# Last down projection of a hybrid trunk computed in two parts of the tokens (320, then 256), with the final norm of the first part beside the second

## The reference, cut to what matters

```
h = rmsnorm(x, p["ffn_norm"][layer])
up = h @ p["w_up"][layer]
c, fb = causal_dwconv(up, ffn_bufs[layer], p["ffn_conv_w"][layer], p["ffn_conv_b"][layer])
x = x + (jax.nn.silu(c[..., :D_FF]) * c[..., D_FF:]) @ p["w_down"][layer]
...
y = rmsnorm(x, p["final_norm"])
```

## Time and profile before

| | |
|---|---|
| median of three runs | 1219.53 us (1217.68 to 1220.73) |
| the profiled execution's own time | 1217.85 us |
| its span in the trace | 1216.1 us |
| TensorE matmul busy | 1186.7 us, 98% of the span |
| VectorE, ScalarE, GpSimd busy | 734.8, 514.8, 615.8 us |
| first matmul of the last down projection | 1159.37 us into the span |
| its last matmul's result taken by VectorE | 1201.60 us |
| last store issued | 1209.31 us |

### The profile page before, as it was taken

How to read it: one execution, slowest core, us unless ns; L and a number is a source line. 1 busy time by engine, 2 the same in 40 slices (tenths; PEclk the granted TensorE clock), 3 DMA queues, 4 the chain that set the end, 5 groups by cost and what they waited for, 6 DMA issues and landing times.

```text
span 1216.1 us, 21634 instructions
## 1 busy us (share of the span) xinstructions
PE 1186.7 (98%) x8636; PEld 1156.6 (95%) x8636; DVE 734.8 (60%) x1468; ACT 514.8 (42%) x881; POOL 615.8 (51%) x628
## 2 busy tenths in 40 slices
PE   7999999999999999999999999999999999999996
PEld 7887899999999999999999999999999999999996
DVE  5999556567845688455512754355785557855542
ACT  6333455444334454343522533344443444533354
POOL 4643435347954469542454323434588355874430
PEclk9999999999999999999999999999999999999998
DMA  6311134221342203422422222322223221232212
GB/s 239 111 36 26 44 81 135 91 69 35 105 139 70 83 22 105 140 74 66 124 85 87 69 80 70 121 71 70 69 71 139 70 83 56 70 139 82 67 40 78
DMA packets 33652, 103.74 MB, mean 85 GB/s; under 512 B 4880, under 2 KB 6928, under 8 KB 33552
## 3 DMA queue, kind: packets, MB, share of 16 engines
q1 hardware_dynamic: 29344, 98.40, 24.8%
q10 hardware_dynamic: 4224, 4.22, 1.1%
HBM read 98.29 MB, written 4.79 MB: 85 GB/s over the span
## 4 chain that ended last, share of the span: by engine, by line
PE 80%; DVE 9%; ACT 4%; POOL 4%; issue 2%; DMA 1%; ACTq 0%; SPq 0%; DVEq 0%
PE psum L398 62%; PE psum L593 12%; PE psum L494 3%; POOL w_lo L1259 2%; DVE psum L1749 2%; DVE psum L1637 2%; DVE block_lo L1637 2%; ACT psum L1022 1%; ACT w_hi L950 1%; DVE squares_sum L1848 1%; PE psum L438 1%; PE psum L673 1%; PE psum L446 0%; POOL arena L1274 0%; POOL w_raw L1285 0%
## 5 line engine op out<-in xcount | busy, mean ns | idle before, releaser
L398 PE MATMUL psum<-x_hi,w_hi 128*128 128x288 f32 x1856 | 401.8, 298 | 6.8 <-ACT w_hi L741 6.8
L398 PE MATMUL psum<-x_hi,w_lo 128*128 128x288 f32 x1856 | 398.5, 296 | 1.1 <-POOL w_lo L1179 1.1
L398 PE MATMUL psum<-x_lo,w_hi 128*128 128x288 f32 x1856 | 398.3, 296 | 0.0
L1179 POOL TENSOR_TENSOR w_lo<-w_raw,w_hi 128x1024 fp32r<-128x1024 f32 (+2 forms) x104 | 231.0, 2226 | 277.5 <-ACT w_hi L741 277.4
L398 PEld LDWEIGHTS psum<-x_hi,w_hi 128*128 128x128 f32 x1856 | 299.9, 189 | 9.0 <-ACT w_hi L741 6.8
L398 PEld LDWEIGHTS psum<-x_hi,w_lo 128*128 128x128 f32 x1856 | 299.9, 189 | 1.5 <-POOL w_lo L1179 1.5
L398 PEld LDWEIGHTS psum<-x_lo,w_hi 128*128 128x128 f32 x1856 | 300.0, 189 | 0.0
L1749 DVE SCALAR_TENSOR_TENSOR psum<-arena,params,psum 128x608 f32<-128x608 f32 x176 | 150.6, 855 | 88.5 <-ACT psum L1022 84.2
L1179 POOL TENSOR_TENSOR w_lo<-arena,w_hi 128x1024 fp32r<-128x1024 f32 (+1 forms) x52 | 120.2, 2311 | 131.7 <-ACT w_hi L741 131.7
L593 PE MATMUL psum<-block_hi,w_hi 128*128 128x288 f32 x448 | 132.7, 296 | 7.0 <-POOL w_lo L1259 7.0
L741 ACT ACTIVATE w_hi<-w_raw 128x1024 fp32r<-128x1024 f32 (+2 forms) x104 | 100.3, 969 | 88.5 <-PE psum L398 78.5
(11 more groups left out here) (184 smaller groups left out, 1502.3 us busy)
## 6 DMA issues: line engine op xcount, KB each, us to landing
w_raw<-in_w_up SPq DMA_DIRECT2D x44, 512.0 KB, 3.3
arena<-in_w_up SPq DMA_DIRECT2D x44, 512.0 KB, 3.3
w_raw<-in_w_down SPq DMA_DIRECT2D x16, 512.0 KB, 3.6
arena<-in_w_down SPq DMA_DIRECT2D x16, 512.0 KB, 3.7
w_raw<-in_w_in_c SPq DMA_DIRECT2D x16, 512.0 KB, 3.2
w_raw<-in_w_in_ab SPq DMA_DIRECT2D x12, 512.0 KB, 3.7
w_raw<-in_w_out_ab SPq DMA_DIRECT2D x16, 256.0 KB, 2.6
w_raw<-in_w_out_c SPq DMA_DIRECT2D x8, 512.0 KB, 3.3
```

The source lines that it names most:

```text
L398: last = nc.tensor.matmul(PS[:, 2 * (q % 2 if slot is None else slot) + half, 0:HALF], w[q][:, k * P:(k + 1) * P], r[:, r_at, half * HALF: ...
L1179: nc.gpsimd.tensor_tensor(w_lo[slot][:, 0:nk * P], raws[RAW_SLOT[RAW[u]]][:, 0:nk * P], w_hi[slot][:, 0:nk * P].bitcast(F32), ALU.subtract ...
```

## The change

The last down projection is computed in two passes over the same eight weight blocks: first for the 320 tokens 256 to 575 (output blocks 2, 3 and the samples), then for the tokens 0 to 255 (blocks 0 and 1). Each of the 16 units `n` writes one PSUM bank (`n % 4`) by 18 matmuls of 320 or 256 columns. All eight split weights have to stay for the second pass: four in `w_hi`/`w_lo`, four in `xh`/`xl`, which the last up unit has left free. The row sums, root, reciprocal, scaling (by GpSimd) and stores of the first part stand beside the second part's matmuls. The transposed tiles are now copied by VectorE, and two banks alternate for them. The last tile's gain is done by VectorE, and in the second part the last 128 features of a row are scaled straight from PSUM.

The diff, cut:

```
+    LAST = (((P * 2, T), range(2, RT)), ((0, P * 2), range(2)))
...
+            for n in range(4):
+                pe.wait_ge(lo_ready, ud + n + 1)
+                pe.wait_ge(acc_free, ud - 1 + n // 2)
+                pe.wait_ge(h_lo_ready, H_FFN[1] + nt - 1)
+                last_products(n, range(nt - 1))
+            pe.wait_ge(h_lo_ready, H_FFN[1] + nt)
+            for n in range(4):
+                last_products(n, [nt - 1]).then_inc(unit_done, 1)
+            for n in range(4, 2 * KD):
+                if n < KD:
+                    pe.wait_ge(lo_ready, ud + n + 1)
+                pe.wait_ge(acc_free, ud + n - 3)
+                last_products(n, range(nt // 2))
+                for q in ((0, 1) if n == 4 else (2, 3) if n == 5 else (n - 2,)):
+                    out_rows(q)
+                if n == KD + 1:
+                    pe.wait_ge(sq_added, (KD - 1) * 4 + KD - 2)
+                    row_sums(sqacc, final=False, rows=LAST[0][1])
+                    pe.wait_ge(sq_ready, KD * 5)
+                    row_sums(sq[:, 1, :], first=False, rows=LAST[0][1]).then_inc(var_mm, 1)
+                last_products(n, range(nt // 2, nt)).then_inc(unit_done, 1)
+            out_rows(2 * KD - 2)
...
+            def out_rows(n):
+                pe.wait_ge(*((xg_ready, n + 1) if n < 2 * KD - 1 else (xg_last, 1)))
+                if n >= 2:
+                    pe.wait_ge(yrow_ready, n - 1)
...
+            def last_stage(ud):          # ScalarE
+                for n in range(2 * KD):
+                    for q in range(2 * n + 3, min(2 * n + 5, KD)):
+                        last_split(ud, q)
...
+                    act.wait_ge(acc_free, ud + n + 1)
...
+                    nc.scalar.activation(sqacc[:, lo:hi] if m == 0 else sq[:, m % 2, lo:hi], X[:, m, lo:hi],
+                                         ACT.Square).then_inc(sq_ready, 1)
+                    if n < 2 * KD - 1:
+                        if n >= 2:
+                            act.wait_ge(y_T, n - 1)
+                        nc.scalar.activation(xg[:, n % 2, lo:hi], X[:, m, lo:hi], ACT.Identity, bias=0.0,
+                                             scale=pcol("final_norm", m)).then_inc(xg_ready, 1)
...
+                for n in range(2 * KD - 1):   # VectorE
+                    last_residual(n)
+                    for q in (() if n < 4 else (0, 1) if n == 4 else (2, 3) if n == 5 else (n - 2,)):
+                        take_rows(q)
+                    if n % KD not in (0, KD - 1):
+                        last_square(n)
+                    if n == KD + 2:
+                        last_factors(0)
...
+            pool.wait_ge(rinv_ready, 7)
+            pool.wait_ge(yrow_ready, KD)
+            for r in LAST[0][1]:
+                rows = y_rows[:, r, :]
+                nc.gpsimd.tensor_scalar(rows, rows, rinv[:, r:r + 1], None, ALU.mult).then_inc(y_row_done, 1)
```

More of the change, by code:

```diff
@@ L249, in hybrid_trunk @@
         u2 = back_raw[:, 0, :]
+        KL = GROUPS[-1][1] * P
+        last_hi, last_lo = ([w[m][:, :] for m in range(4)]
+                            + [v[:, :, :].rearrange("p k t -> p (k t)")[:, m * KL:(m + 1) * KL] for m in range(4)] for w, v in ((w_hi, xh), (w_lo, xl)))
         xg = cut(0, 2, T)
@@ L432, in two_units, with row_sums @@
                     products((u + q) % 4, nk - 1, nk - 1, nk, rh, rl, False, True).then_inc(unit_done, 1)
-            def row_sums(src, first=True, final=True, bank=S0, at=0):
-                for r in range(RT):
+            def row_sums(src, first=True, final=True, bank=S0, at=0, rows=range(RT)):
+                for r in rows:
                     lo = r * P if r < CH else T - P
                     last = nc.tensor.matmul(PS[:, bank, at + r:at + r + 1], src[:, lo:lo + P], ones[:, 0:1],
-                                            start=(first and r == 0), stop=(final and r == RT - 1),
+                                            start=(first and r == rows[0]), stop=(final and r == rows[-1]),
                                             skip_group_check=True)
@@ L627, in ffn @@
                             unit(q, ud + 4 + q, nt, hh, hl)
[L629 to L637, removed]
+            def out_rows(n):
+                pe.wait_ge(*((xg_ready, n + 1) if n < 2 * KD - 1 else (xg_last, 1)))
+                if n >= 2:
+                    pe.wait_ge(yrow_ready, n - 1)
+                for a, r in enumerate(LAST[n // KD][1]):
+                    lo = r * P if r < CH else T - P
+                    last = nc.tensor.transpose(PS[:, M0 + n % 2, a * P:(a + 1) * P], xg[:, n % 2, lo:lo + P], ident[:, :])
+                last.then_inc(y_T, 1)
             ffn(0)
@@ L716, in _, with last_products @@
             nt = GROUPS[-1][1]
[L717 to L725, removed]
+            def last_products(n, ks):
+                m, (lo, hi) = n % KD, LAST[n // KD][0]
+                for k in ks:
+                    for a, (ws, rs) in enumerate(((last_hi, hh), (last_hi, hl), (last_lo, hh))):
+                        last = nc.tensor.matmul(PS[:, n % 4, 0:hi - lo], ws[m][:, k * P:(k + 1) * P], rs[:, k, lo:hi],
+                                                start=(k == 0 and a == 0), stop=(k == nt - 1 and a == 2))
+                return last
+            for n in range(4):
[20 more added lines that the diff above has]
+            out_rows(2 * KD - 2)
+            pe.wait_ge(sq_added, (KD - 1) * 4 + 2 * (KD - 2))
+            row_sums(sqacc, final=False, bank=S1, rows=LAST[1][1])
+            pe.wait_ge(sq_ready, KD * 6)
+            row_sums(sq[:, 1, :], first=False, bank=S1, rows=LAST[1][1]).then_inc(var_mm, 1)
+            out_rows(2 * KD - 1)
         @block.scalar
@@ L1058, in ffn @@
                             norm_in(2, m, r + 1, "mix_norm", KD + m)
[L1059 to L1065, removed]
@@ L1076, in _, with last_root @@
+            def last_root(part, bank):
+                act.wait_ge(var_mm, 7 + part)
+                a, b = LAST[part][1][0], LAST[part][1][-1] + 1
+                nc.scalar.activation(std[:, a:b], PS[:, bank, a:b], ACT.Sqrt, bias=eps[:, 0:1], scale=1.0 / D)\
+                    .then_inc(std_ready, 1)
             ffn(0)
```

133 lines of the change are left out of this document (95 added, 38 removed).

## The result

The changed kernel took 1222.95 us (median of 5 runs, 1221.71 to 1226.31). The kernel before took 1219.07 us beside it (5 runs, 1217.68 to 1220.73). The ratio is 1.0039, with a 95% interval of 1.0026 to 1.0052: slower by 0.39%. (The two medians alone are 0.32% apart; the ratio and its interval come from all the runs.) The forecast was 1222.6 us, slower by 0.25%. The profiled execution took 1221.71 us, with a span of 1220.0 us and a mean granted clock of 0.997.

What follows compares the result with a forecast made beforehand. TensorE, busy for 98% of the span, bounds the kernel, with a 14.5 us tail to shorten. +10.0 us up to its last result and -6.9 in the tail give +3.1: 1222.6 us (+0.25%), range 1218.5 to 1227.

Steps and rivals of the forecast that it cites:

- The matmuls: Last down projection: 320 and 256 columns cost 146.7 and 120.0 ns, sum 38.4 us as before, no change.
- the rival with narrow matmuls at 110 ns: Last down projection: matmuls get cheaper, 133.3 and 110 ns; +0.2 us with all waits, 1215.5 us without two; chance 0.10.
- First wait: Before the fourth unit, TensorE waits for GpSimd's low part of the fourth weight block: 3.3 us instead of 0.3, +3.0 us.
- Second wait: In the middle of unit 4, TensorE waits for ScalarE's gain of the second tile: +1.3 us.
- Third wait: In the middle of unit 5, TensorE waits for VectorE's copy, queued behind sums that wait for GpSimd: +3.35 us.
- The small waits: After unit 5's wait, TensorE waits 0.1 to 0.2 us for each of the next copies: +0.3 us.
- More work ahead of the last matmul: On TensorE: 36 transposes instead of 30, +0.66 us, and 12 passes of first-part row sums, +1.4 us.
- The tail: From TensorE's last result to the program's end: 7.6 us instead of 14.5, -6.9 us, allowing 6.6 to 8.4.
- The last result: TensorE's last large matmul result comes at 1211.6 us instead of 1201.6, +10.0 us.
- the clock as a case by itself: Rival: TensorE's clock falls in the 3.3 us waits, 2.0 us per fall; 1224.6 us with one, 1226.6 both; chance 0.32.
- the prediction's own sign of being wrong: A granted TensorE clock under 1.00 between 1165 and 1211 us would show the forecast wrong.
- The rival that the second and third wait are mostly absent: Units 4 and 5: 2.25 to 4 us of waiting go, +0.8 to -0.9 us, 1218.6 to 1220.3 us; chance 0.20.

Runs made afterwards that it cites:

- the fourth split early: Changed kernel, but ScalarE splits the fourth weight block before rounding the last hidden tile instead of behind the table load; 1219.26 us, ratio 1.0000.
- ScalarE's row: Changed kernel, but at the end ScalarE scales all 896 SBUF columns of output block 1 and GpSimd none; 1221.62 us, ratio 1.0033.
- the filled waits: Changed kernel plus unread 320-column matmuls, 18 before the fourth unit and 15 in the middle of unit 5; 1220.90 us, ratio 1.0012.
- all splits before the squares: Changed kernel, but ScalarE makes all five late weight splits in one go ahead of the first square; 1220.29 us, ratio 1.0013.
- the squares in PSUM: Changed kernel, but ScalarE writes the squares of tiles 1 to 4 to PSUM, where VectorE's sums read them; 1220.37 us, ratio 1.0007.
- the early splits: Changed kernel, but blocks 4 to 6 are split before the last product's high part, 7 and 8 right behind the table load; 1212.75 us, ratio 0.9964.
- the profile taken again: The changed kernel itself run once more, unaltered, beside the kernel before; 1221.39 us, ratio 1.0033.
- the last kernel: Changed kernel with the early splits and ScalarE's row, plus first-part sums one residual later and two copies ahead of the fifth residual; 1213.82 us, ratio 0.9949.
- the early splits with ScalarE's row taken again: Changed kernel with the early splits and ScalarE's row together, run again in a later job; 1214.29 us, ratio 0.9956.

## Why the prediction came out as it did

The path, its waits and the shorter tail came as predicted. Slower by 0.25% was forecast and 0.39% measured, so the measured ratio lies just beyond the 0.3% that can be told from no change (its interval, 0.26 to 0.52%, reaches below), where the forecast lay just within. Point by point:

- **The matmuls.** 147 and 117 to 119 ns were measured, against 146.7 and 120.0. That the sum doesn't change held, and the rival with narrow matmuls at 110 ns fell.
- **First wait.** 2.97 us against 3.3, in the named place with the named releaser. It is additive, as the experiment with the fourth split early showed.
- **Second wait.** 0.85 us against 1.3.
- **Third wait.** 2.55 us against 3.35: the mechanism was right and its size was off. The prediction let each sum hold up GpSimd's next block by 0.5 us, a figure read off a sum of 576 columns, where these have 320. The two blocks that came behind a sum lost 0.25 us each. So the sums came 2.1 us apart and not 2.3. They took 1.1 us each, where the prediction named 1.5 or more as a sign of being right. On the clock of before (0.62 us taken off) TensorE reached the wait at 1179.0, predicted 1179.2, and went on at 1181.6, predicted 1182.6: an earlier copy makes up the 0.8 us.
- **The small waits** of 0.3 us did not come.
- **More work ahead of the last matmul.** Transposes 0.11 us each, as taken; row sums 1.23 us against 1.4.
- **The tail.** 7.7 us against 7.6. GpSimd's 384 columns took 1.50 us, where the prediction said at most 0.92 by the row of the 768-wide subtraction: that bound was wrong. It cost little, 0.17 us by the experiment with ScalarE's row, since only ScalarE's store waits for them. The hold of VectorE's 896 columns that the range allowed for did not come (0.68 us with GpSimd's piece and without).
- **The last result.** 52.3 us after the stage's start, 52.2 predicted. This agreement is luck, since two errors cancel. Waits were taken 1.9 us too long (8.25 us in place of 6.37), and the clock's fall, 1.4 us by the filled waits, stood in a rival and not in the forecast.

So the step that failed in the form of the forecast is the clock as a case by itself, weighed at 0.32 against the rest. A clock below 1.00 between 1165 and 1211 us was the prediction's own sign of being wrong, and it came. It is a part of the forecast's own path: in each of the six profiles with an unfilled wait of 2.5 us or more (the changed kernel's two, the fourth split early, all splits before the squares, the squares in PSUM, ScalarE's row) the clock was below 1.00 somewhere in the stage. In the filled waits, and in the four profiles with the early splits, whose longest wait ahead of the tail is 0.9 us, it stayed at 1.00 until the tail. The price of a fall was put at 2.0 us; 1.4 us was measured for the one in the profile after, about 1.1 for the second one beside ScalarE's row. In the profile taken again the stage was 0.9 us longer, though its waits were 0.5 us shorter, so that longer fall cost about 1.4 us more, 2.8 in all; by the means of the stretches it lasted about twice as long.

The rival that the second and third wait are mostly absent fell: they are 3.4 us, and that VectorE's sums and GpSimd's subtractions hold each other up is shown by the squares in PSUM.

Of the sum, about 0.5 us of the stage's growth is assigned to no row: from the stage's start to the last result it is 10.0 us more (52.3 - 42.2), less 6.1 of waits, 0.7 of transposes, 1.2 of row sums and 1.4 to 1.6 of the clock. The 0.6 us upstream are no more than runs of one kernel vary by.

## What to carry to other kernels

When a change makes a consumer start on more blocks sooner, move their producers with it: the two parts shortened the tail by 6.8 us as meant, and moving five ScalarE instructions of 0.8 us ahead of where they stood turned +0.33% into -0.36%. Ask of each helper engine's queue what runs beside it: VectorE's sums of two SBUF operands took 0.6 us more beside GpSimd's subtractions, next to nothing more beside its multiplications (0.43 us, one 0.58), and no more than alone once they came after them or had an operand in PSUM. And where a change adds waits of 2.5 to 3 us on TensorE, the stretch at the lower clock behind them belongs in the sum and not in a case by itself.

## What the runs showed that I had not expected

- **The clock falls behind some waits, and not the same ones each time.** In the profile after it stayed up behind 2.97 us and fell behind 2.55; taken again, it fell behind the first and not the third. Behind waits of 1.8 us in the block products, near 450 and 1045 us, it stayed up in the profiles of the kernel before and of the changed one, and fell in those of the filled waits (above) and of the last kernel (0.83 in both stretches); near 450 us alone it fell with the squares in PSUM and in the early splits with ScalarE's row taken again (0.83). Runs of the kernel before alone reached from 1216.9 to 1221.5 us in one job, with mean clocks that fall from 0.996 to 0.992 as the time grows (34 of 35 runs; one has 0.945 at 1219.9 us), and from 1216.5 to 1217.8 in the next, which ran on another chip. What decides it is open, the chip included, and so is whether it alone makes the runs of a kernel differ.
- **GpSimd's multiplication by one factor per partition is dear.** Three rows of 1024 columns took 8.50 us, 2.83 each, and 384 columns took 1.50, about 2.8 to 3.9 ns a column. Its subtraction of two operands, at 768 columns in 1.84 us, is 2.4 ns a column. VectorE worked beside each of these multiplications (a sum of squares in each row, its own 896 columns beside the 384), so how much of their time is waiting for VectorE is not shown.
